# One whole block pair per feed-forward layer, all full norms by products with ones, and the norm's split moved

## The chip, the cores and the metric

The kernel runs on one core of a Trainium2 chip. The metric is device time in microseconds. The engines named below are PE (the matmul engine), DVE (vector), ACT (scalar), POOL (GpSimd) and SP (which issues the weight loads).

## What is computed

512 tokens of width 1024 pass through two chained models. The first has two layers: a gated recurrent mixer with memory attention (block A), then band attention with memory attention (block B), each followed by a feed-forward part with a causal convolution of three taps on the gate half. The second model has one layer (block C: two kinds of attention) and a plain gated feed-forward part. Every stage starts with a norm over the width. Cut to what matters here:

```
def rmsnorm(x, g):            # x32 * rsqrt(mean(x32 * x32) + eps) * g
def conv_ffn(h, w_up, conv_w, conv_b, w_down):        # layers 0 and 1, d_ff = 2816
    u, g = split(h @ w_up)
    g = g[t] * w2 + g[t-1] * w1 + g[t-2] * w0 + b     # causal_dwconv, k = 3
    return (silu(g) * u) @ w_down
second model, layer "2":      x = x + (silu(h2 @ w_gate) * (h2 @ w_up)) @ w_down
x = x + mixer(rmsnorm(x));  x = x + conv_ffn(rmsnorm(x));  k, v = rmsnorm(x, kv_g) @ w_kv
```

## The kernel before

**Layout.** Activations are held transposed, X[:, k, :] being features 128k to 128k+127 by 512 tokens. Every fp32 product is made of three products of rounded parts: high x high, high x low, low x high. The high part is a copy on ACT (`hH`, `WH`, `FH`, `TH`, `accH`), the low part a subtraction on DVE (`hL`, `WL`, `FL`, `TL`, `accL`). Weights come by SP's loads into `raw`; a unit of 2048 columns is converted in two halves (step `conv`), a chunk of 1024 in one (`cconv`).

**Feed-forward layers.** The 2816 hidden features are 11 block pairs of 256 gate and 256 up columns. The first WHOLE[i] pairs of layer i are computed whole: tiles g0, g1, u0, u1, each of 24 products of 512 columns (L1489; g1 in two halves, L1508, with the norm's products between). The other pairs use Winograd's form: seven products of half the width and half the depth (order 1, 5, 6, 3, 7, 2, 4; each 24 products of 256 columns, L1838). Their right operands are input sums T made by the steps `wtB`, `wtS`, `wtL` (four short DVE sums at L2557 to L2568, a copy, a low part at L2575; p = 0 to 3) and `wt7` (high and low of T7). Their left operands are weight blocks or sums of them (`wsum`, L2539, then `cconv`). Products 1, 6, 7, 4 share one PSUM bank: before 6, 7 and 4 the bank must be copied out by ACT (`wcopy`, tiles held, L2055); 5 and 3 share another. The down projection runs in pieces of 24 products (`wd`, L1864) that wait for the low part FL of the hidden tiles they read; ACT copies them out (`wx`) and POOL adds them to X by DMA.

**A whole pair's pointwise chain**: `wg0` (DVE, times the norm's R; in layers 0 and 1 then ACT's Identity with the last tap and the bias), `wt0` (in layers 0 and 1 two tap products per tile on DVE at L2601, then ACT's Silu), `wy0` (times R), `wu0` (times u; after the second tile ACT's FH), `wlast` (FL of the last whole pair).

**Norms.** ACT squares each X tile; POOL (in the residual steps of A, B, C and layer 0) or DVE adds the squares into acc. Two forms then follow. By rows (`row_split`, `row_sums`, `row_inverse`, for the names in ROW_NORMS): accH and accL, two PE products with a matrix of ones (L1378), a Sqrt over 128 x 512 on ACT (L2139), a reciprocal over 128 x 512 on DVE (L2734). By columns (`rstd_first`, `rstd_second`, used at n2): PE sums to four columns (L1371), a Sqrt and a reciprocal of 128 x 4, PE spreads them (L1383), ACT copies to Rsb.

**Order.** `order()` writes one list of steps, and each engine executes its own part of it strictly in that order; semaphores join the engines. `conv_ahead` puts conversions as far ahead as the four half-slots of converted weights allow. In a Winograd layer, `later(...)` lists groups of steps, and one group is put behind each product or down piece. `tile_done` puts norm steps and timed steps (gates) behind tiles. A `fence` makes the engines wait for each other's latest marked work; the one named acc2 stands ahead of layer 1, with a small load (graw) on ACT and a small weight copy on DVE (gw) behind it.

Of the kernel before, what the change touches and what calls it, by code (L numbers as in the profile page):

```python
# [10 lines left out]
ALU = mybir.AluOpType  # L11
# [22 lines left out]
NSU = 11  # L34
WHOLE = (2, 2, 1)
CHUNK = 1024
# [284 lines left out]
def pieces(hd):  # L321
# [3 lines left out]
    if hd % 2 == 0:  # L325
# [11 lines left out]
             "C": ([4, 5, 0, 1, 2, 3, 6, 7], 6)}  # L337
ROW_NORMS = ("ffn0", "kv", "ffn1")
NEXT_NORM = {"A": "ffn0", "B": "ffn1", "C": "n2"}
# [8 lines left out]
def order():  # L348
# [56 lines left out]
    def sink(*x):  # L405
        put(*x)
        if x[0] == "conv_in":
            deferred.append(("silu", x[1], x[2]))
        if x[0] == "gate":
            timed.extend([[1, ("gates_later",)], [3, ("gates_sums",)], [4, ("gates_rest",)], [6, ("gate_columns",)], [7, ("m_rows",)]])  # L410
        if x[0] == "fg":
            timed.extend([[0, ("fg_later",)], [1, ("fg_rest",)], [3, ("rows",)]])
        if x[0] == "rope":
            timed.append([1, ("rope_later", x[1], x[2])])
# [86 lines left out]
    def rstd(i, eps):  # L501
        norms.extend([("row_split", i), ("row_sums", i, eps), ("row_inverse", i)])

# [85 lines left out]
    def ffn_wino(i, end):  # L589
# [27 lines left out]
        def half(m, n, x):  # L617
            put("fm_half", f"g{i}", m, n, 128 * (m % 2), st, x)

        n = take()  # L620
        whole("g", 0, n)
        if st in ROW_NORMS:
            put("row_split", st)
            put("wtS", i, 1)
            half(1, n, 0)
            put("row_sums", st, 60)
            put("wtL", i, 1)
            half(1, n, 1)
            put("row_inverse", st)
            put("wtB", i, 2)  # L630
            put("wtS", i, 2)
        else:
            put("rstd_first", st, 61)
            put("wtS", i, 1)
            put("wtL", i, 1)
            put("wtB", i, 2)
            put("wtS", i, 2)
            whole("g", 1, n)
            put("rstd_second", st)
        done.add(n)  # L640
# [18 lines left out]
        if WHOLE[i] == 1:  # L659
            conv_ahead(len(UNITS))  # L660
            for m in (0, 1):
                put("wt0", f"g{i}", m)
            put("wy0", i, 0)
        conv_ahead(len(UNITS))
# [22 lines left out]
        if WHOLE[i] == 2:  # L687
            later([], [("wu0", f"u{i}", 3)], [("wt7", i)], [("wlast", i, 1)])
        else:
            later([("wt7", i)], [("wu0", f"u{i}", 0)], [("wu0", f"u{i}", 1)], [("wlast", i, 0)])  # L690
        for x in SEQUENCE[i]:
# [166 lines left out]
    ffn(0, "ffn0", "kv")  # L858
    put("sqrt_table", "kv")
    fm(1, "mix1", "qB", "R")  # L860
    put("fence", "kv")
# [147 lines left out]
def program(nc, wall, xt, memt, colsd, biasd, consts, rope, gatew, out):  # L1009
    ctx = ExitStack()  # L1010
    with ctx:
# [1450 lines left out]
        def vector(e):  # L2462
# [44 lines left out]
            for what, *a in STEPS:  # L2507
# [485 lines left out]
                elif what == "res_last":  # L2993
                    low_part(a[0], 7, col(a[0], 7))

                elif what == "g":
# [181 lines left out]
        def gpsimd(e):  # L3178
            w, mark = Lane(e), partial(ev.mark, "pool")

            for what, *a in STEPS:
# [66 lines left out]
                elif what == "res_norm":  # L3248
                    stage, m, st = a
                    if m:  # L3250
                        w.wait_ge(*at("sqA", st, m))
                        w.wait_ge(*(at("accP", st, m - 1) if m > 1 else at("sqA", st, 0)))
                        e.tensor_tensor(acc[:, :], acc[:, :], sq[m % 2][:, :], ALU.add).then_inc(
                            *mark("accP", st, m))
# [63 lines left out]
        def sync(e):  # L3318
# [34 lines left out]
            for h, k, n in STORES:  # L3353
# [9 lines left out]
        FFN_NEXT = ["kv", "n1", "last"]  # L3363
        SQ_LAST = {"mix0": "D", "ffn0": "P", "kv": "P", "ffn1": "P", "n2": "P", "last": "D"}
        R_OF["qmB"] = R_OF["qB"] = "kv"
# [7 lines left out]
        RCOL_USED = {"mix0": [], "kv": [("vev", "vA", 2, 2)], "n1": [("vev", "vB", 2, 2)],  # L3373
                     "n2": [("vev", "fv", 2, 1)], "last": [("spread", "n2")]}

# [129 lines left out]
```

## Time and profile before

| | us |
|---|---|
| median of 3 runs | 1774.73 (1773.79 to 1775.9) |
| profiled execution, its own time | 1773.94 |
| span of its trace | 1772.2 |
| PE busy | 1758.5 (99%) |
| DVE busy | 1293.8 (73%) |
| ACT busy | 950.0 (54%) |
| POOL busy | 205.3 (12%) |

PE's granted clock is full (0.999) over the span. In the rows, times are us from the span's start, then the duration; xN is a count; a bracket gives the idle time before the instruction and what released it. Busy PE time counts overlapping products; the distance between starts is the pace. Layer 0's feed-forward part starts at 260.2, layer 1's at 828.5, layer 2's at 1416.6; block B starts at 606.1, block C at 1177.5.

### The profile page before, as it was taken

To read this page: it belongs to the slowest core of one execution; us is meant where nothing else is said; L and a number is where in the kernel's file an instruction comes from. 1 tells how busy PE (TensorE), PEld (TensorE's weight loads), DVE (VectorE), ACT (ScalarE), POOL (GpSimd) and SP (SyncE) were. 2 spreads that over 40 slices of the span, in tenths; PEclk is the share of its full clock that TensorE was granted. 3 is DMA by queue.
4 is the path that set the end of the run, shared out by engine and by line. 5 is a ranking of instruction groups with operands and counts; after the bars stand their busy time and mean duration, and the time that the engine had idled before them with its cause. 6 is when DMAs were issued, how large, how long until landed. Compare 5 with 4: busy or idle time off the path is not lost.

```text
span 1772.2 us, 26238 instructions
## 1 busy us (share of the span) xinstructions
PE 1758.5 (99%) x10680; PEld 1525.7 (86%) x10680; DVE 1293.8 (73%) x1791; ACT 950.0 (54%) x1440; POOL 205.3 (12%) x226
## 2 busy tenths in 40 slices
PE   9999999999999999999999999999999999999998
PEld 7877788999999887787899999977777899999997
DVE  6878568888786765646888788689767487766766
ACT  6645444655554544754465555552567455454454
POOL 0001220110111200002011010103001101111110
PEclk9999999999999999999999999999999999999999
DMA  6231223654554342212264554443221235555442
GB/s 250 72 94 62 71 96 107 155 141 134 142 136 127 97 149 99 96 49 94 90 176 117 155 130 134 118 118 108 72 96 48 98 105 145 141 142 144 108 137 78
DMA packets 61623, 205.19 MB, mean 116 GB/s; under 512 B 7344, under 2 KB 9520, under 8 KB 53184
## 3 DMA queue, kind: packets, MB, share of 16 engines
q1 hardware_dynamic: 38832, 162.55, 27.6%
q0 software_dynamic: 17280, 31.46, 10.0%
q10 hardware_dynamic: 5392, 9.51, 1.7%
q8 instruction: 85, 1.39, 0.3%
q14 instruction: 34, 0.28, 0.0%
HBM read 169.38 MB, written 2.13 MB: 97 GB/s over the span
## 4 chain that ended last, share of the span: by engine, by line
PE 89%; DVE 6%; ACT 3%; issue 1%; DMA 1%; POOL 0%; ACTq 0%; DVEq 0%; SPq 0%; POOLq 0%
PE ps L1838 31%; PE ps L1489 17%; PE ps L1864 16%; PE ps L1403 6%; PE ps L1528 4%; PE ps L1651 2%; PE ps L1548 2%; PE ps L1696 2%; PE ps L1676 2%; DVE WL L2523 2%; PE ps L1735 1%; PE ps L1887 1%; PE ps L1716 1%; ACT WH L1978 1%; PE ps L1905 1%
## 5 line engine op out<-in xcount | busy, mean ns | idle before, releaser
L1838 PE MATMUL ps<-hH,WH 128*128 128x256 f32 x896 | 253.6, 283 | 0.7 <-ACT held L2055 0.7
L1838 PE MATMUL ps<-hH,WL 128*128 128x256 f32 x896 | 253.6, 283 | 0.0
L1838 PE MATMUL ps<-hL,WH 128*128 128x256 f32 x896 | 253.5, 283 | 0.0
L2545 DVE TENSOR_TENSOR WL<-raw,WH 128x1024 fp32r<-128x1024 f32 x138 | 168.1, 1220 | 112.8 <-ACT WH L1989 112.8
L2523 DVE TENSOR_TENSOR WL<-raw,WH 128x1024 fp32r<-128x1024 f32 (+1 forms) x137 | 169.4, 1275 | 83.8 <-ACT WH L1978 83.6
L1489 PE MATMUL ps<-hH,WH 128*128 128x512 f32 x528 | 208.3, 395 | 0.0
L1489 PE MATMUL ps<-hH,WL 128*128 128x512 f32 x528 | 205.7, 389 | 0.0
L1489 PE MATMUL ps<-hL,WH 128*128 128x512 f32 x528 | 205.6, 389 | 0.0
L3277 POOL DMA_DIRECT2D X<-sq x120 | 104.9, 964 | 862.4 <-ACT sq L2044 860.7
L1838 PE MATMUL ps<-TH,WL 128*128 128x256 f32 x672 | 190.2, 283 | 0.0
L1838 PE MATMUL ps<-TL,WH 128*128 128x256 f32 x672 | 190.2, 283 | 0.0
L1838 PE MATMUL ps<-TH,WH 128*128 128x256 f32 x672 | 190.1, 283 | 0.0
L2545 DVE TENSOR_TENSOR WL<-Wsum,WH 128x1024 fp32r<-128x1024 f32 x112 | 136.7, 1221 | 68.0 <-ACT WH L1989 67.9
L1978 ACT ACTIVATE WH<-raw 128x1024 fp32r<-128x1024 f32 (+1 forms) x137 | 134.4, 1028 | 83.9 <-PE ps L1489 44.2
L1838 PEld LDWEIGHTS ps<-hH,WH 128*128 128x128 f32 x896 | 171.9, 192 | 2.1 <-ACT held L2055 0.9
L1838 PEld LDWEIGHTS ps<-hL,WH 128*128 128x128 f32 x896 | 171.9, 192 | 1.2
L1838 PEld LDWEIGHTS ps<-hH,WL 128*128 128x128 f32 x896 | 171.9, 192 | 0.0
L1864 PE MATMUL ps<-FH,WH 128*128 128x512 f32 x432 | 168.7, 391 | 0.0
L1864 PE MATMUL ps<-FL,WH 128*128 128x512 f32 x432 | 168.7, 390 | 0.0
L1864 PE MATMUL ps<-FH,WL 128*128 128x512 f32 x432 | 168.1, 389 | 0.0
L1989 ACT ACTIVATE WH<-raw 128x1024 fp32r<-128x1024 f32 x138 | 144.5, 1053 | 18.7 <-PE ps L1838 16.5
L1989 ACT ACTIVATE WH<-Wsum 128x1024 fp32r<-128x1024 f32 x112 | 117.9, 1054 | 55.7 <-PE ps L1838 43.0
(442 smaller groups left out, 3890.8 us busy)
## 6 DMA issues: line engine op xcount, KB each, us to landing
raw<-in_wall SPq DMA_DIRECT2D x166, 512.0 KB, 4.4
raw<-in_wall SPq DMA_DIRECT2D x65, 1024.0 KB, 4.8
X<-sq POOLq DMA_DIRECT2D x120, 256.0 KB, 4.0
bias<-in_bias ACTq DMA_DIRECT2D x12, 256.0 KB, 2.9
raw<-in_wall SPq DMA_DIRECT2D x8, 256.0 KB, 6.6
X<-in_xt SPq DMA_DIRECT2D x8, 256.0 KB, 7.3
CB<-rows ACTq DMA_DIRECT2D x8, 256.0 KB, 3.3
out_y<-X SPq DMA_DIRECT2D x8, 256.0 KB, 2.2
```

What stands on the lines that cost most here:

```text
L1403: mm = e.matmul(ps[b][:, :], ww[:, k, c:c + 128], x, start=(k == seq[0] and i == 0), stop=(k == seq[-1] and i == 2))
L1489: mm = e.matmul(ps[b][:, 0:N], ww[:, k, c:c + 128], x[:, k, 0:N], start=(k == 0 and i == 0), stop=(k == 7 and i == 2))
L1528: mm = e.matmul(o, x[:, k, t * 128:t * 128 + 128], ww[:, k, :], start=(k == 0 and i == 0), stop=(k == 7 and i == 2))
L1548: mm = e.matmul(ps[b][:, :], x[:, k, t * 128:t * 128 + 128], ww[:, kx, :], start=(k == 0 and i == 0), stop=(k == 7 and i == 2))
L1651: mm = e.matmul(ps[b][:, c:c + L], queries[u["kind"]][r, u["m"], t * 128:t * 128 + 128], keys[u["kind"]][r, u["m"], 0:L], start=opens, sto ...
L1838: mm = e.matmul(ps[b][:, 256 * u:256 * u + 256], ww[:, p, 128 * u:128 * u + 128], x, start=(opens and p == 0 and u == 0 and n == 0), stop= ...
L1864: mm = e.matmul(ps[BANK["wd", i, g, m]][:, :], ww[:, kx, mi * 128:mi * 128 + 128], x[:, f % 8, :], start=(kx == 0 and n == 0), stop=(kx == ...
L1978: e.activation(WH[W_AT["unit", n] // 2][:, c], unit_raw(n)[:, c], ACT.Copy).then_inc(*mark("wh", n, x))
L1989: e.activation(chunk_slot(c)[0], chunk_src(c), ACT.Copy).then_inc(*mark("wh", "c", c))
L2523: e.tensor_tensor(WL[v][:, c], unit_raw(n)[:, c], WH[v][:, c].bitcast(F32), ALU.subtract).then_inc(*mark("wl", n, x))
L2545: e.tensor_tensor(L, chunk_src(c), H.bitcast(F32), ALU.subtract).then_inc(*mark("wl", "c", c))
L3277: e.dma_start(X[:, m, :], part[m % 2][:, :], accum_op=ALU.add).then_inc(s_part[m % 2], 16)
```

## The change

Layers 0 and 1 have one whole pair instead of two (layer 2 had one already), so ten Winograd blocks instead of nine. Their whole pair's taps, Silu, times R and times u are put behind the first Winograd products by `later`. The norm n2 is made by rows, as ffn0, ffn1 and kv were. At ffn0, ffn1 and n2 the last square is added by DVE instead of POOL, the split (accH, accL) stands ahead of the next unit's conversion instead of behind the first tile, and the Sqrt table is loaded ahead. At kv the split stands between the two halves of a conversion. The gate steps of block C (`fg_later`, `fg_rest`, `rows`) come one tile later.

```
-WHOLE = (2, 2, 1)
+WHOLE = (1, 1, 1)
-ROW_NORMS = ("ffn0", "kv", "ffn1")
+ROW_NORMS = ("ffn0", "kv", "ffn1", "n2")
-            timed.extend([[0, ("fg_later",)], [1, ("fg_rest",)], [3, ("rows",)]])
+            timed.extend([[1, ("fg_later",)], [2, ("fg_rest",)], [4, ("rows",)]])
     def rstd(i, eps):
-        norms.extend([("row_split", i), ("row_sums", i, eps), ("row_inverse", i)])
+        norms.extend([None, ("row_sums", i, eps), ("row_inverse", i)])
...
+        put("row_split", st)
         n = take()
+        put("sqrt_table", st)
         whole("g", 0, n)
-        if st in ROW_NORMS:
-            put("row_split", st)
-            ...
-        else:
-            put("rstd_first", st, 61)
-            ...
-            put("rstd_second", st)
+        put("wtS", i, 1)
+        half(1, n, 0)
+        put("row_sums", st, 61 if i == 2 else 60)
+        put("wtL", i, 1)
+        half(1, n, 1)
+        put("row_inverse", st)
+        put("wtB", i, 2)
+        put("wtS", i, 2)
         done.add(n)
         if WHOLE[i] == 1:
             sum_ahead(i)
...
         if WHOLE[i] == 1:
             conv_ahead(len(UNITS))
-            for m in (0, 1):
-                put("wt0", f"g{i}", m)
-            put("wy0", i, 0)
+            if i == 2:
+                for m in (0, 1):
+                    put("wt0", f"g{i}", m)
+                put("wy0", i, 0)
...
+        elif i == 2:
+            later([("wt7", i)], [("wu0", f"u{i}", 0)], [("wu0", f"u{i}", 1)], [("wlast", i, 0)])
         else:
-            later([("wt7", i)], [("wu0", f"u{i}", 0)], [("wu0", f"u{i}", 1)], [("wlast", i, 0)])
+            later([("wt7", i)], [("wt0", f"g{i}", 0), ("wt0", f"g{i}", 1)], [("wy0", i, 0), ("wu0", f"u{i}", 0)],
+                  [("wu0", f"u{i}", 1)], [("wlast", i, 0)])
...
     ffn(0, "ffn0", "kv")
     put("sqrt_table", "kv")
+    _, n = ITEMS[now["conv"]]
+    put("conv", n, 0)
+    put("row_split", "kv")
+    put("conv", n, 1)
+    now["conv"] += 1
     fm(1, "mix1", "qB", "R")
...
                 elif what == "res_last":                      # vector
                     low_part(a[0], 7, col(a[0], 7))
+                    w.wait_ge(*at("sqA", a[0], 7))
+                    w.wait_ge(*at("accP", a[0], 6))
+                    e.tensor_tensor(acc[:, :], acc[:, :], sq[1][:, :], ALU.add).then_inc(*mark("accD", a[0], 7))
...
                 elif what == "res_norm":                      # gpsimd
-                    if m:
+                    if 0 < m < 7:
```

The tables SQ_LAST and RCOL_USED follow (who adds the last square, and who last read the columns).

## Rows read from the trace of the kernel before

**Rows 1.** The page's first part: busy us, share, instructions.
```profile
PE 1758.5 (99%) x10680; PEld 1525.7 (86%) x10680; DVE 1293.8 (73%) x1791; ACT 950.0 (54%) x1440; POOL 205.3 (12%) x226
```
**Rows 2.** The chain of waits in order of time: start, us, what.
```profile
271.68 32.64 PE ps L1489 x144
...
394.66 14.39 PE ps L1838 x120
409.05 5.47 PE ps L1864 x24
```
**Rows 3.** Timeline of PE around norms and gates: start, us, what, idle before.
```profile
260.18 0.39 PE L1489 MATMUL ps<-hH,WH 128*128 128x512 f32 x1
...
268.34 0.39 PE L1378 MATMUL ps<-accH,ones_r 128*128 128x512 f32 x1
...
271.52 0.39 PE L1489 MATMUL ps<-hH,WH 128*128 128x512 f32 x1
...
617.98 0.47 PE L1378 MATMUL ps<-accH,ones_r 128*128 128x512 f32 x1 [0.86 <-DVE accL L2480]
...
838.62 0.47 PE L1378 MATMUL ps<-accH,ones_r 128*128 128x512 f32 x1 [1.82 <-DVE accL L2480]
...
889.50 0.39 PE L1838 MATMUL ps<-hH,WH 128*128 128x256 f32 x1 [0.72 <-ACT held L2055]
...
1197.63 1.02 PE L1915 MATMUL ps<-Gf,gsum 128*8 128x512 f32 x2 [0.62 <-DVE Gf L2467]
...
1416.57 0.39 PE L1489 MATMUL ps<-hH,WH 128*128 128x512 f32 x1
...
1429.21 0.48 PE L1489 MATMUL ps<-hH,WH 128*128 128x512 f32 x1
```
**Rows 4.** Windows: stretch, us, busy of PE, PEld, DVE, ACT, POOL, then clock, DMA.
```profile
304.00:335.00 31.00, 31.00 (x217) 29.07 (x216) 26.42 (x26) 18.49 (x26) 6.21 (x7) 1.00 0.57 136
...
1416.00:1440.00 24.00, 24.00 (x116) 20.11 (x115) 22.40 (x31) 11.66 (x16) 3.28 (x2) 1.00 0.26 88
```
**Rows 5.** Timelines of DVE and POOL at the kv norm and layer 1's.
```profile
617.15 0.69 DVE L2480 TENSOR_TENSOR accL<-acc,accH 128x512 fp32r<-128x512 f32 x1
...
830.00 3.41 POOL L3253 TENSOR_TENSOR acc<-acc,sq 128x512 f32<-128x512 f32 x2 [4.32 <-ACT sq L2330]
...
835.37 0.22 DVE L2772 TENSOR_TENSOR gw<-graw,gg 128x64 f32<-128x64 f32 x1 [1.61 <-DMA graw<-in_gatew]
...
837.79 0.68 DVE L2480 TENSOR_TENSOR accL<-acc,accH 128x512 fp32r<-128x512 f32 x1
```
**Rows 6.** Durations, from DVE's timeline and the page's groups (busy, mean ns, idle).
```profile
271.67 3.35 DVE L2734 RECIPROCAL Rsb<-Rsb 128x512 f32<-128x512 f32 x1 [1.04 <-ACT Rsb L2139]
...
282.75 2.98 DVE L2601 SCALAR_TENSOR_TENSOR yz<-gs,cols,yz 128x511 f32<-128x511 f32 x4 [0.29 <-ACT yz L2018]
...
1425.00 0.48 DVE L2568 SCALAR_TENSOR_TENSOR Tf<-X,small,Tf 128x256 f32<-128x256 f32 x1
...
L2545 DVE TENSOR_TENSOR WL<-raw,WH 128x1024 fp32r<-128x1024 f32 x138 | 168.1, 1220 | 112.8 <-ACT WH L1989 112.8
...
L1989 ACT ACTIVATE WH<-raw 128x1024 fp32r<-128x1024 f32 x138 | 144.5, 1053 | 18.7 <-PE ps L1838 16.5
```
**Rows 7.** Timelines of DVE, PE and ACT in the head of layer 2.
```profile
1420.26 3.45 DVE L2523 TENSOR_TENSOR WL<-raw,WH 128x1024 fp32r<-128x1024 f32 x2
...
1434.08 0.95 DVE L2575 TENSOR_TENSOR TL<-Tf,TH 128x768 fp32r<-128x768 f32 x1
1434.94 1.22 DVE L2545 TENSOR_TENSOR WL<-raw,WH 128x1024 fp32r<-128x1024 f32 x1
...
1440.19 0.28 PE L1838 MATMUL ps<-hH,WH 128*128 128x256 f32 x1
...
1442.50 1.28 ACT L2026 ACT_TABLE_LOAD   x1
1443.79 1.15 ACT L2026 ACTIVATE yz<-gs 128x512 f32<-128x512 f32 x2
```

## What was predicted

> **What bounds the kernel now.** I read the page first. PE is busy 99% of the span at full granted clock, the vector engine (DVE) 73% [rows 1]. The chain of waits is PE almost throughout, and in the steady part of a feed-forward layer nothing else appears: five Winograd products take 14.39 us, a down piece 5.47 [rows 2]. So the time can fall only by fewer PE columns or by closing one of the few PE gaps, and it rises by whatever makes PE wait. Then I read the PE timeline around the norms: the products with ones have no gap in layer 0, 0.86 us at the kv norm, 1.82 at layer 1 [rows 3]. Last, the window table: DVE is busy 26.4 of 31 us from 304 to 335 and 22.4 of 24 in the head of layer 2, which already has one whole pair [rows 4]. DVE is thus the engine to watch when work is pulled together.
>
> **PE work removed.** A whole pair is four tiles of 24 products, 96 x 0.2267 = 21.76 us (32.64 / 144 is the 0.2267). A Winograd block is seven times 24 half-width products, 7 x 2.878 = 20.15 us (14.39 / 5) [rows 2]. One pair is exchanged in layers 0 and 1: 1.61 x 2 = **-3.2 us**. The down pieces stay the same.
>
> **PE gaps closed.** Without a gap, two tiles and the two products with ones take 2 x 5.44 + 0.46 = 11.34 us: in layer 0 exactly from 260.18 to 271.52 [rows 2, 3]. A gap costs its idle time and about 0.24 for the refill: products of 0.39 us are issued 0.23 apart, so 0.16 of overlap is lost, and the first one after the gap takes 0.47 (0.08 more) [rows 3].
> Layer 1: 1.82 idle, 2.1 in all. The products wait for accL, which DVE makes at 837.79, behind two WL halves, themselves behind the small weight copy that waits for a DMA until 835.37 [rows 3, 5]. Now the seventh square is added by DVE (0.68) after the sixth, whose POOL add I put at 831.8, the middle of the 3.41 us for two; the graw load of ACT, now held by the fence until POOL's last add ends at 833.4 [rows 5], leaves about 0.6 us sooner (832.9) and lands near 834.75, and accL is next, done at 835.6. PE asks for it at 836.6. Gap gone: **-2.1**. The two WL halves behind it end at 837.9 and are wanted at 839.8: covered.
> Kv norm: 0.86 idle, 1.1 in all. Both splits now sit between the halves of the next conversion: accH after the first WH (614.83) and after POOL's last add, accL ends near 616.7 instead of 617.84 [rows 3, 5]. PE would ask for it near 617.0 (1.0 before 617.98). **-1.1**; the second WL half moves by 0.7 and is first read 2.7 us into the next tile.
> Layer 2: 1416.57 to 1429.21 is 12.64, with 16 small products; with the new form 11.34: **-1.3** [rows 3].
> Gate sums of block C: they move one tile (5.7 us) later, past Gf, so the 0.62 us gap [rows 3] closes: **-0.6** (the refill left out, since the two small products have one anyway). The Exp, Ln and the row store move with them by one tile; their reader is the fox part, tens of us later, so nothing is charged.
> A gap of 0.72 in layer 1 at 889.50 (q3 behind a held copy) [rows 3] lies in the stretch that is replaced: **-0.9** with the refill.
> Together **-9.2 us**.
>
> **What the change adds, in the DVE queue.** DVE and ACT run strictly in step order, so I lay the new order out, each item starting when the one before it ends (0.08 us overlap on DVE, 0.10 on ACT, as rows that follow each other show) or 0.04 after what it waits for; PE starts 0.15 after WL. Durations: a 1024-wide sum or low part 1.22, four T sums of 0.48 with their waits 1.75, the reciprocal 3.35, four taps 2.98, and on ACT a WH 1.05 [rows 6]; the 512-wide steps are half of these or a little more (0.68), a pair of 512-wide ones 1.28. Laid over the old order of layer 2, this gives 1434.7 for the end of the last TL, and the row has 1435.03 [rows 7].
>
> Layer 0, new order. DVE: low parts 6 and 7 to 262.6, square add to 263.2, ACT accH, accL to 264.6, two WL to 267.2, T sums to 268.9, TL 1 to 270.8, reciprocal to 274.0, T sums to 275.7, Wsum to 276.9, TL 2 to 277.7, T sums to 279.5, Wsum to 280.7, TL 3 to 281.5, WL of q1 to 282.7. PE has finished the u pair at 271.52 + 10.88 = 282.4 and starts q1 at 282.8: a wait of 0.4. Then WL q5, two gs, Wsum, WL q6 (0.9 late, ACT does the Identity pair first), Wsum, WL q3, L7, WL q7 to 292.7, the taps to 295.6. On ACT the step "taps behind the second copy" puts both Silus after held q5 and **ahead of** WH q2 and held q6: the second Silu ends at 296.2, WH q2 at 297.2, held q6 at 297.7. PE has done q1, q5, q6, q3 by 294.3, and q7 writes into the bank that held q6 empties: it starts at 297.8, a wait of **3.5**. q2 ends at 303.6. The down piece needs FL of the whole pair: DVE does WL q2 (298.4), times R (299.6), two u products (302.0, the d piece's WL between them); ACT FH to 303.1 and WH q4 to 304.1; DVE WL q4 to 305.4 and only then FL to 306.5. The piece starts at 306.6: a wait of **3.1**. In the old order the second whole pair (21.8 us of PE against some 13 us of DVE) paid for all this. After s = 1 DVE needs about 26 of 31 us per block [rows 4] and I find no further wait. Layer 0: **7.0 us**.
>
> Layer 1 is the same, but DVE stands at the weight copy until about 835.0, so WL q1 ends at 853.3 and PE is ready at 850.7: 2.8 + 3.5 + 3.1 = **9.4 us**.
>
> Layer 2 has no taps and kept its single pair; there WL q1 ended at 1436.16 and q1 began at 1440.19, 4.0 us of cover [rows 7]. The new norm adds to DVE the square add 0.6, accL with the wait for accH 1.4 and the reciprocal 3.35 - 0.16, while PE comes 1.4 us sooner; back come about 1.1 us that two WL lost beside POOL's add (3.45 us, where two of 1.22 take 2.36) and nearly as much in the low part before them [rows 6, 7]. The layout gives WL q1 at 1440.1 against PE at 1438.8: 1.4, and q6 waits 1.5 more for held q1, which ACT does behind a WH (waiting for its Wsum), the table load and two Silus. **2.9 us**.
>
> Bounds of these unshown waits: below, 0 in all, no wait, the old head of layer 2 being the nearest row; at durations 3% shorter I get 15.6 us, at 3% longer 22.8; the value taken is 19.3, since the same layout lags the old trace rather than leads it.
>
> ACT's table: the trace has the load at 1442.50 for 1.28 us and the next Silu at 1443.79 [rows 7]. The Trainium skill, "ScalarE: Activation LUTs" (What ACT_TABLE_LOAD costs), adds a drain of 1.38 us to every switch; here the next instruction follows at once. By the page the q6 wait of layer 2 would grow by 1.4 (in layers 0 and 1 the Silu waits for the taps anyway) and the time would be 1786.2; I go by the row.
>
> **Sum.** Own time of the profiled execution 1773.94 - 9.2 + 19.3 = 1784.0; the median of the runs lies 0.8 above that execution, so **1784.8 us**.
>
> **Rivals.**
> *The cover holds (faster).* No wait appears at the heads: 1774.7 - 9.2 = **1765.5**. For it: layer 2 ran its single whole pair without a PE gap, and DVE is idle 27% of the span [rows 1]. Against: that head had no taps (2.98), no reciprocal (3.35), and DVE was busy 22.4 of 24 us. It decides if the waits total under 9.2 us. Chance 0.10.
> *Half of them.* The q7 waits don't arise (held q6 gets through before the Silus) and layer 2 keeps its cover: 19.3 - 7.0 - 2.9 = 9.4 of waits, net +0.2: **1774.9**. Against: ACT executes in order, and the Silus stand first. Chance 0.08.
> *More waiting.* DVE or the loads run late: at 3% longer durations +13.6, and if the loads of the first parts gate Wsum (raw slots are released by the two WL that now end 0.8 later) another 1 to 2: **1789**. For it: the trace runs up to 1 us behind my layout near POOL adds. Against: POOL adds less now. Chance 0.17.
> *The gaps don't close* (the norm products still wait, because accL is late again): -9.2 shrinks by up to 3.2: **1788**. Chance 0.05.
> *The forecast:* 0.60, own range 1780 to 1788.
>
> **Range and chances.** The lower end takes in the half case, the upper the two worse ones: 1775 to 1790. Under 0.2% (3.5 us) a run can't be told from no change. Faster 0.11, same 0.07, slower 0.82.
>
> **What would show it.** Right: no PE gap at the products with ones at kv and layer 1; in layers 0 and 1 a PE gap of 3 to 4 us released by an ACT held copy before product 7 (the fifth in order), one of about 3 us before the first down piece released by DVE FL, a smaller one at q1; in layer 2 two of about 1.5; L1838 with 168 x 2 more products, L1489 with 96 x 2 fewer; POOL one add fewer at three norms. Wrong: heads without gaps, or DVE idle over 3 us between the reciprocal and the taps in layer 0; or new gaps in the middle of the layers, where I have none.

## The result, and the profile of the changed kernel

The changed kernel takes 1786.38 us (median of 4 runs, 1785.71 to 1787.97), the kernel before beside it 1774.26 (1773.02 to 1775.9): the ratio is 1.0071, 95% interval 1.006 to 1.0083. It is slower by 12.1 us. The forecast was 1784.8, that is 10.1 above the 1774.73 from which it started. A second measurement of the same kernel gave 1786.23 and 1.0067 [1.0055, 1.008].

The page's first part, to be held against [rows 1], and its slices of the granted clock:

```profile
PE 1761.6 (99%) x10810; PEld 1535.7 (86%) x10810; DVE 1316.2 (74%) x1813; ACT 961.1 (54%) x1455; POOL 202.5 (11%) x223
...
PEclk9999999999999999999899999999999999999999
```

PE is busy 3.1 us longer, though 3.2 us of its work were taken out: a product at a lower clock counts as busy for longer. One slice is an 8, the one that holds the head of layer 1. No slice of the kernel before was below 9. The counts are as forecast: 336 more products at the Winograd line (5040 for 4704); 216 fewer at the line of the whole tiles, of which 192 are the two pairs and 24 are layer 2's g1, now made in halves at another line; three adds fewer on POOL.

The PE timeline at the five places of [rows 3] and at the heads of the three feed-forward layers (start, us, what, idle before):

```profile
282.95 0.35 PE L1839 MATMUL ps<-hH,WH 128*128 128x256 f32 x1 [0.71 <-DVE WL L2546]
...
298.01 0.58 PE L1839 MATMUL ps<-hH,WH 128*128 128x256 f32 x1 [3.33 <-ACT held L2056]
...
307.04 0.47 PE L1865 MATMUL ps<-FH,WH 128*128 128x512 f32 x1 [1.50 <-DVE FL L2694]
...
622.43 0.39 PE L1379 MATMUL ps<-accH,ones_r 128*128 128x512 f32 x1
...
841.01 0.39 PE L1379 MATMUL ps<-accH,ones_r 128*128 128x512 f32 x1
...
858.48 0.56 PE L1839 MATMUL ps<-hH,WH 128*128 128x256 f32 x1 [3.26 <-DVE WL L2546]
...
873.54 0.39 PE L1839 MATMUL ps<-hH,WH 128*128 128x256 f32 x1 [0.59 <-ACT held L2056]
...
882.56 0.77 PE L1865 MATMUL ps<-FH,WH 128*128 128x512 f32 x1 [3.01 <-DVE FL L2694]
...
1214.96 1.03 PE L1916 MATMUL ps<-Gf,gsum 128*8 128x512 f32 x2
...
1452.43 0.36 PE L1839 MATMUL ps<-hH,WH 128*128 128x256 f32 x1 [1.60 <-DVE WL L2546]
...
1459.85 0.39 PE L1839 MATMUL ps<-TH,WH 128*128 128x256 f32 x1 [1.43 <-ACT held L2056]
```

A row without a bracket had no idle time before it: the gaps of 0.86 (kv norm), 1.82 (layer 1's norm) and 0.62 (gate sums) of [rows 3] are gone, and the 0.72 too. Eight new ones stand in the three heads: before product 1 (q1), before product 7 (q7; in layer 2 product 6), before the first down piece. Together 15.4 us.

Two of the queues behind these gaps, both in layer 0. ACT ahead of product 7: the second Silu, the WH of product 2, then the copy that product 7 waits for:

```profile
295.90 0.63 ACT L2027 ACTIVATE yz<-yz 128x512 f32<-128x512 f32 x1 [0.82 <-DVE yz L2602]
296.44 1.04 ACT L1990 ACTIVATE WH<-raw 128x1024 fp32r<-128x1024 f32 x1
297.38 0.58 ACT L2056 ACTIVATE held<-ps 128x512 f32<-128x512 f32 x1
```

DVE ahead of the first down piece: a WL that waits for ACT, then FL:

```profile
304.53 1.23 DVE L2546 TENSOR_TENSOR WL<-raw,WH 128x1024 fp32r<-128x1024 f32 x1 [1.54 <-ACT WH L1990]
305.67 1.22 DVE L2694 TENSOR_TENSOR FL<-yz,FH 128x1024 fp32r<-128x1024 f32 x1
```

What the gaps don't show is in the windows of the same kernel (stretch, us, busy of PE, PEld, DVE, ACT, POOL, granted clock, DMA share, GB/s):

```profile
290.00:298.00 8.00, 4.69 (x40) 4.48 (x38) 6.29 (x8) 5.16 (x8) 0.00 (x0) 1.00 0.39 131
298.00:307.00 9.00, 7.53 (x48) 7.33 (x48) 7.36 (x9) 4.34 (x5) 0.00 (x0) 0.81 0.46 123
...
858.00:862.00 4.00, 3.52 (x16) 3.55 (x17) 3.80 (x5) 1.89 (x3) 0.00 (x0) 0.50 0.00 0
862.00:866.00 4.00, 4.00 (x26) 4.00 (x25) 3.36 (x3) 3.54 (x5) 0.00 (x0) 0.67 0.02 4
866.00:870.00 4.00, 4.00 (x35) 4.00 (x35) 3.96 (x6) 2.37 (x4) 0.00 (x0) 1.00 0.78 262
882.00:886.00 4.00, 3.44 (x8) 2.80 (x9) 3.97 (x5) 1.06 (x1) 0.00 (x0) 0.50 0.45 131
886.00:891.00 5.00, 5.00 (x19) 4.00 (x19) 4.93 (x7) 2.49 (x4) 1.77 (x2) 0.75 0.11 20
```

A clock between 0.50 and 1.00 is the mean over a stretch that holds both levels. Behind each gap of 3 us the granted clock is at 0.50, the lower level of 1.2 GHz, and is back at 1.00 some 3 to 6 us after the gap. PE counts as busy there, but the window from 858, idle only in its first 0.48 us, holds 16 products where the one from 866 holds 35. The first four products of layer 1 took 14.47 us for 11.7 in layer 0, its first down piece 8.48 for 5.73.

By stage of the profiled execution: layer 0 +5.8 us, block B with the kv norm -1.1, layer 1 +8.2, block C -0.7, layer 2 to the end +2.1, the start -0.3. That is +14.0 in the span; this execution is the slowest of its four, 1.6 above their median.

### The profile page after: what moved, and what is told of

Read it like the earlier page. It is cut to its first block, busy times and chain, and to the rows that moved or that the text cites. A ratio compares the mean times of both kernels' runs of the same rounds, so it can differ in the third digit from the quotient of the medians.

```text
span 1786.2 us, 26555 instructions
## 1 busy us (share of the span) xinstructions
PE 1761.6 (99%) x10810; PEld 1535.7 (86%) x10810; DVE 1316.2 (74%) x1813; ACT 961.1 (54%) x1455; POOL 202.5 (11%) x223
## 4 chain that ended last, share of the span: by engine, by line
PE 88%; DVE 6%; ACT 3%; issue 1%; DMA 0%; DVEq 0%; SPq 0%; ACTq 0%
PE ps L1839 32%; PE ps L1865 17%; PE ps L1490 15%; PE ps L1404 5%; PE ps L1529 4%; PE ps L1888 3%; PE ps L1549 2%; PE ps L1652 2%; PE ps L1697 2%; PE ps L1677 2%; DVE WL L2524 1%; PE ps L1736 1%; DVE WL L2546 1%; PE ps L1717 1%; PE ps L1906 1%
## 5 line engine op out<-in xcount | busy, mean ns | idle before, releaser
L1839 PE MATMUL ps<-hH,WH 128*128 128x256 f32 x960 | 274.3, 286 | 9.5 <-DVE WL L2546 5.6
L1839 PE MATMUL ps<-hH,WL 128*128 128x256 f32 x960 | 273.8, 285 | 0.0
L1839 PE MATMUL ps<-hL,WH 128*128 128x256 f32 x960 | 273.8, 285 | 0.0
L1839 PE MATMUL ps<-TH,WH 128*128 128x256 f32 x720 | 204.3, 284 | 1.4 <-ACT held L2056 1.4
L1839 PEld LDWEIGHTS ps<-hH,WH 128*128 128x128 f32 x960 | 186.3, 194 | 12.1 <-issue 6.7
L1839 PEld LDWEIGHTS ps<-hL,WH 128*128 128x128 f32 x960 | 186.3, 194 | 1.0
L1839 PEld LDWEIGHTS ps<-hH,WL 128*128 128x128 f32 x960 | 186.3, 194 | 0.0
L1490 PE MATMUL ps<-hH,WH 128*128 128x512 f32 x456 | 180.4, 396 | 0.0
L1490 PE MATMUL ps<-hL,WH 128*128 128x512 f32 x456 | 177.9, 390 | 0.0
L1490 PE MATMUL ps<-hH,WL 128*128 128x512 f32 x456 | 177.8, 390 | 0.0
```

The source lines that it names most:

```text
L1490: mm = e.matmul(ps[b][:, 0:N], ww[:, k, c:c + 128], x[:, k, 0:N], start=(k == 0 and i == 0), stop=(k == 7 and i == 2))
L1839: mm = e.matmul(ps[b][:, 256 * u:256 * u + 256], ww[:, p, 128 * u:128 * u + 128], x, start=(opens and p == 0 and u == 0 and n == 0), stop= ...
```

## The experiments

Theory: the loss is the waits at the heads of the layers. They come from the order and the fullness of the DVE and ACT queues when one whole pair, not two, covers them, and the lowered clock behind them enlarges them. Rivals: the norm edits cost; the clock costs nothing of its own; DVE has no room in any order. Eleven variants and the changed kernel again were run. To compare them, this is the stretch from the end of the last u product to the end of the first down piece, in one profiled execution each, with one product (2.9) taken off where product 4 stands inside. The gaps are those before q1, before q7 and before the down piece, with the one before product 4 (q4) where it is named. Its work alone is 6 x 2.88 + 5.47 = 22.7 us.

| kernel | layer 0: gaps; stretch | layer 1: gaps; stretch | median us |
|---|---|---|---|
| changed | 0.71, 3.33, 1.50; 30.5 | 3.26, 0.59, 3.01; 35.8 | 1786.4 |
| changed_again | 0.71, 3.31, 1.56; 30.5 | 2.59, 1.83, 3.01; 33.9 | 1786.2 |
| pairs_only | 1.22, 3.32, 0.49; 31.0 | 0.64, 3.32, 0.39; 30.4 | 1785.1 |
| gate_load_later | 0.72, 3.31, 1.68; 30.5 | 1.68, 3.32, 0.41; 31.5 | 1784.3 |
| filled_gaps_layer1 | 0.73, 3.32, 1.53; 30.5 | 4.2 (filled 2.9), 1.76, 0.26; 32.4 | 1785.2 |
| taps_behind_q6 | 0.73, 0, 8.32; 34.1 | 2.68, 0, 6.83; 36.9 | 1792.7 |
| silus_behind_q6 | 0.72, 0, 4.84; 31.2 | 2.67, 0, 3.36; 32.2 | 1785.6 |
| taps_and_down_later | 0.73, 0, 5.43; 31.3 | 3.38, 0, 4.11; 33.6 | 1787.2 |
| order_mended | 0.72, 0, 2.83 (q4), 0; 28.2 | 1.62, 0, 2.84 (q4), 0; 30.3 | 1780.5 |
| mended_old_n2 | 0.72, 0, 2.84 (q4), 0; 28.2 | 1.68, 0, 2.84 (q4), 0; 29.2 | 1778.9 |
| mended_twice | 0.71, 0, 0, 1.55; 25.5 | 1.68, 0, 0, 1.53; 26.4 | 1778.6 |

**norms_only.** The norm edits and the new split order without the exchange in layers 0 and 1.

```
-WHOLE = (1, 1, 1)
+WHOLE = (2, 2, 1)
```

> The changed kernel with the split order and the norm edits, but layers 0 and 1 keep two whole pairs. Theory (the time is lost at the heads with one whole pair, the norm edits are worth what the gaps closed): block B -1.1, layer 1 norm -2.1, layer 2 norm form -1.3, gate sums -0.6, and the two new waits at the head of layer 2 +3.5 as the changed kernel's trace shows them: about 1.6 us under the kernel before, 1772.7. Rival (the norm edits themselves cost, by DVE work at the heads of all layers): above 1776. Rival (the whole loss comes from the pairs and layer 2's waits too need them): under 1770.5.

Measured 1773.68, ratio to the kernel before 0.9997 [0.9988, 1.0005], medians 0.9 us apart, which is not clear of the noise. The expectation was 1.6 faster; both rivals are out. Of the eight new gaps only layer 2's two are left, as PE's timeline shows:

```profile
1437.41 0.36 PE L1839 MATMUL ps<-hH,WH 128*128 128x256 f32 x1 [1.58 <-DVE WL L2546]
...
1444.82 0.39 PE L1839 MATMUL ps<-TH,WH 128*128 128x256 f32 x1 [1.43 <-ACT held L2056]
```

**norms_old_n2.** In addition layer 2's norm by columns again.

```
-ROW_NORMS = ("ffn0", "kv", "ffn1", "n2")
+ROW_NORMS = ("ffn0", "kv", "ffn1")
+        (for n2: rstd_first / rstd_second, last square on POOL, as before)
```

> As norms_only, and the norm of layer 2 again by small products over columns, its last square added by POOL. Theory: layer 2's two waits (3.5) and its gain (1.3) both go, so -1.1 -2.1 -0.6 = 3.8 us under the kernel before, 1770.5, and 2.2 under norms_only. Rival (layer 2's waits are not owed to its norm form): no difference from norms_only.

Measured 1771.04, ratio 0.9982 [0.9974, 0.9991]: 3.6 under the kernel before (3.8 expected) and 2.6 under norms_only (2.2). No gap over 0.05 us is left between 1400 and 1460. So layer 2's two waits belong to its new norm form, and this is the version that beats both kernels. No run takes the norm edits apart: whether the square on DVE or the earlier split closed layer 1's gap is not shown.

**pairs_only.** The exchange of the pairs alone, on the kernel before.

```
-WHOLE = (2, 2, 1)
+WHOLE = (1, 1, 1)
+        (taps and their followers by later(), as in the changed kernel)
```

> The kernel before with one whole pair in layers 0 and 1 and their taps behind the first product copies; norms and split order as before. Theory: the waits at the heads of layers 0 and 1 come from the order of the DVE and ACT queues there and stand without the norm edits: -1.6 x 2 - 0.9 + 7.9 + about 12 = +16, 1790. Rival (the waits need the norm edits, whose reciprocal and square add push the queue late): under 1782.

Measured 1785.11, ratio 1.0065 [1.0052, 1.0078]: +10.5, not +16, and not under 1782. The mechanism stands without the norm edits. Layer 0 lost 8.3 for 7.9 expected, layer 1 7.7 for 12. PE's timeline of this kernel, of layer 0 and of layer 1's norm:

```profile
298.94 0.58 PE L1842 MATMUL ps<-hH,WH 128*128 128x256 f32 x1 [3.32 <-ACT held L2059]
...
843.92 0.67 PE L1382 MATMUL ps<-accH,ones_r 128*128 128x512 f32 x1 [1.85 <-DVE accL L2484]
```

The norm's gap of 1.85 is there again, and behind it q1 of layer 1 waits only 0.64 us; in the changed kernel the norm has no gap and q1 waits 3.26 or 2.59. The two waits together are 2.5 us here and 2.6 or 3.3 there, so with one whole pair what is gained at that norm is given back at q1. That accounts for most of the 2.5 us by which the two parts alone, +10.5 and -0.9, fall short of the 12.1 of both.

**gate_load_later.** The small weight copy for which DVE stood still at layer 1's head is moved into the middle of the layer.

```
-    put("gg")
-    put("gate_weights", "C")
     ffn(1, "ffn1", None)
 ...
+            if (i, s, q) == (1, 2, 6):
+                put("gg")
+                put("gate_load", "C")
+            if (i, s, q) == (1, 2, 4):
+                put("gate_weights", "C")
```

> The changed kernel, but the small gate weights of block C are loaded and scaled in the middle of layer 1 and no longer at its head, so that DVE doesn't stand at 837.4 to 839.8. Theory (a PE gap of about 3 us is followed by a granted clock of 0.50 to 0.67, which costs again as much): WL of q1 comes 2.4 us sooner, the gap before q1 shrinks from 3.3 to about 0.8, PE stays at full clock there, and layer 1 loses what layer 0 does, 7.9 for 13.3: 5 us under the changed kernel, 1781. In the profile: granted clock 1.00 from 858 to 870, and the wait before q7 grows from 0.6 to about 3.3. Rival (the clock costs nothing of its own, only the wait counts): -2.4 or, as the later waits take it up, nothing: 1784 to 1786.

Measured 1784.25, ratio 1.0059 [1.0045, 1.0073]: 2 us under the changed kernel, neither 5 nor nothing. The profile has the things that the theory named, clock 1.00 from 858 to 870 and q7's wait at 3.3, but q1's gap shrank to 1.68 and not to 0.8. PE's timeline, then two windows:

```profile
857.19 0.36 PE L1842 MATMUL ps<-hH,WH 128*128 128x256 f32 x1 [1.68 <-DVE WL L2549]
...
872.25 0.58 PE L1842 MATMUL ps<-hH,WH 128*128 128x256 f32 x1 [3.32 <-ACT held L2059]
```

Columns as in the windows above:

```profile
858.00:862.00 4.00, 4.00 (x36) 4.00 (x35) 3.19 (x5) 3.18 (x4) 0.00 (x0) 1.00 0.01 4
...
870.00:876.00 6.00, 3.75 (x17) 3.75 (x18) 4.26 (x6) 3.00 (x4) 0.00 (x0) 0.61 0.29 87
```

The stretch is 31.5, 4.3 less than in the changed kernel's first profile but 2.4 less than in its second, which is nearer to its median. And the lowered clock moved with the gap, to q7: those 48 products took 8.62 us for 5.9. In the changed kernel DVE stood at the copy as long as this row says:

```profile
839.80 0.23 DVE L2773 TENSOR_TENSOR gw<-graw,gg 128x64 f32<-128x64 f32 x1 [2.44 <-DMA graw<-in_gatew]
```

Without it WL of q1 came 1.6 us sooner, counted from the layer's first product, and not 2.4, because DVE then waits 0.75 us for accH and 0.26 for a WH at the same place.

**changed_again.** The changed kernel once more, to see whether its clock was an accident.

> The changed kernel itself, word for word, beside the others of this call. Its profiled execution lay 1.6 us above its median, so part of the lowered clock in layer 1 may belong to that execution alone. Theory: gaps of 3 us or more always bring a lower clock behind them, but how much it costs changes between executions; median 1786 to 1787, and the profile of this run has granted clocks under 1.00 behind the same gaps. Rival: this profile has 1.00 there; then the lowered clock was an accident of one execution.

Measured 1786.23; the theory holds. The lower clock is behind the same two gaps, but shorter: 0.57 from 858 to 862 and 1.00 from there, 0.59 from 882 to 886. It cost 1.5 us at each where the first profile has 2.7. The gap at q1 is 0.7 shorter, and so is the time for which DVE stood at the weight copy: 1.71 us for 2.44, until its load landed. DVE's timeline:

```profile
839.38 0.23 DVE L2773 TENSOR_TENSOR gw<-graw,gg 128x64 f32<-128x64 f32 x1 [1.71 <-DMA graw<-in_gatew]
```

PE's:

```profile
858.06 0.55 PE L1839 MATMUL ps<-hH,WH 128*128 128x256 f32 x1 [2.59 <-DVE WL L2546]
```

And its windows:

```profile
858.00:862.00 4.00, 3.94 (x20) 3.97 (x21) 3.38 (x4) 2.31 (x3) 0.00 (x0) 0.57 0.00 0
862.00:866.00 4.00, 4.00 (x36) 4.00 (x35) 3.77 (x4) 3.83 (x6) 0.00 (x0) 1.00 0.15 19
```

**filled_gaps_layer1.** Products that nobody reads, where PE stood idle in layer 1 (the operands are abbreviated here).

```
+                    if (i, st, pn) == (1, 1, 1):
+                        w.wait_ge(*at("wh", "c", c))
+                        for n in range(24):
+                            e.matmul(ps[b][:, 0:256], WH of c [:, 0, 0:128], hH[:, 0, 0:256], start=True, stop=True)
 ...
+                        if (i, g, part) == (1, 0, 0) and pair == ms[0:2]:
+                            w.wait_ge(*at("wsilu", "H", i, 0))
+                            for n in range(12):
+                                e.matmul(ps[BANK["wd", i, g, ms[0]]][:, :], W[0][:, 0, 0:128], FH[:, 0, :], start=True, stop=True)
```

> The changed kernel with products that nobody reads, written into the bank that the real ones open afresh behind them: in layer 1, 24 of 128x256 before the wait for WL of q1 and 12 of 128x512 before the wait for FL of the first down piece. PE is busy where it stood idle, nothing else moves. Theory (the clock that falls behind a gap costs about 3 us twice in layer 1): granted clock 1.00 from 858 to 870 and from 882 to 891, 96 products in 11.7 us for 14.5, the down piece in 5.7 for 8.5; the wait before q7, which the slow products had hidden, grows from 0.6 to 3.3: together about 3 us less, 1783.3. Rival (the slow products only fill time that the waits take anyway): the stretch from u's end to the end of the down piece stays 36.0 us and the time 1786.

Measured 1785.24, ratio 1.0064 [1.0049, 1.0079]: 1.0 under the changed kernel's second measurement, less than the 3 expected and inside the spread of that kernel's executions (1784.32 to 1787.0), with these windows:

```profile
858.00:862.00 4.00, 4.00 (x36) 4.00 (x35) 3.40 (x4) 2.30 (x3) 0.00 (x0) 1.00 0.02 4
...
882.00:886.00 4.00, 3.84 (x17) 3.20 (x18) 3.96 (x5) 1.06 (x1) 0.00 (x0) 1.00 0.38 126
```

PE's timeline of the same kernel at q1, the filler and the first real product:

```profile
856.76 3.10 PE L1835 MATMUL ps<-hH,WH 128*128 128x256 f32 x24 [1.25 <-ACT WH L2001]
859.70 0.28 PE L1844 MATMUL ps<-hH,WH 128*128 128x256 f32 x1
```

The clock stays at 1.00, the 96 products take 11.7 and the down piece 5.7: that the clock has a price of its own is shown by these rows, not by the median. But the filler had to wait for WH until 856.76, and the first real product came at 859.70, 1.6 us later than in changed_again (858.06), which gave back half of the gain. Set against changed_again, the stretch is 1.5 shorter, and 3.1 without the overrun.

**taps_behind_q6.** Taps and Silus one step later, behind held q6 (layers 0 and 1).

```
-            later([("wt7", i)], [("wt0", f"g{i}", 0), ("wt0", f"g{i}", 1)], [("wy0", i, 0), ("wu0", f"u{i}", 0)],
+            later([("wt7", i)], [], [("wt0", f"g{i}", 0), ("wt0", f"g{i}", 1)], [("wy0", i, 0), ("wu0", f"u{i}", 0)],
```

> The changed kernel, but in layers 0 and 1 the four taps and two Silus of the whole pair stand one step later, behind the copy that empties product 6's bank (held q6); what follows them moves one step later too. Theory (the wait of 3.3 us before product 7 is only ACT's order): that wait is gone in both layers, but DVE has as much to do before FL, so most of it comes back before the first down piece, where 1.5 us (layer 0) and 3.0 (layer 1) become 4 to 5: 1784 to 1786, 0 to 2 under the changed kernel. Rival (each wait stands for itself): q7's 3.3 + 0.6 and the lowered clock behind them, some 2, are saved: 1780.

Measured 1792.72, ratio 1.0105 [1.0088, 1.0122]: 6 us slower than the changed kernel; both expectations fell. q7's wait is gone, as both said, but FL ended at 308.88 in place of 306.89, and PE stood 8.32 us before the down piece, then ran it at 0.50. The DVE timeline shows who is ahead of FL:

```profile
303.70 0.68 DVE L2618 TENSOR_TENSOR yz<-ps,yz 128x512 f32<-128x512 f32 x1
...
306.52 1.22 DVE L2546 TENSOR_TENSOR WL<-raw,WH 128x1024 fp32r<-128x1024 f32 x1 [0.99 <-ACT WH L1990]
307.66 1.22 DVE L2694 TENSOR_TENSOR FL<-yz,FH 128x1024 fp32r<-128x1024 f32 x1
```

ACT's timeline, with the row for which FL and the WH of that WL both wait:

```profile
304.48 1.06 ACT L2036 ACTIVATE FH<-yz 128x1024 fp32r<-128x1024 f32 x1 [4.18 <-DVE yz L2618]
```

A step later in the list is not one instruction later in the queue. A Wsum and a WL for the next block stand ahead of FL; but a WL that waits for ACT stood there in the changed kernel too, and FL begins 2.1 us behind the end of FH in both. What is new lies ahead of that: DVE did one more WL before the taps and a Winograd sum before the second product with u, which ran at 303.70 in place of 301.71. FH, that WL and FL each came 2.0 us later, while PE, without q7's wait and the slow clock, asked for FL 4.8 us earlier.

**taps_and_down_later.** The same, and the first down piece behind product 4.

```
+for x in SEQUENCE[:2]:
+    j = x.index(("d", 0, 0))
+    x[j:j + 2] = [x[j + 1], x[j]]
```

> As taps_behind_q6, and in layers 0 and 1 the first down piece stands behind product 4, so one more product (2.88 us) covers FL. Theory: no wait before product 7, at most 2 before the down piece, gaps of under 2 us with the clock kept at 1.00 in layer 0: 5 to 8 us under the changed kernel, 1780 with 1778 to 1782. Layer 1 keeps its wait of 3.3 at q1 and the lowered clock behind it. Rival (a DVE backlog that any order meets): within 2 us of the changed kernel.

Measured 1787.17, ratio 1.0074 [1.0059, 1.0089], the rival's answer: product 4 covers 2.9 of the 8.3, and FL, in the same queue, still ends at 308.82.

**silus_behind_q6.** On ACT alone; DVE's order is that of the changed kernel.

```
-            later([("wt7", i)], [("wt0", f"g{i}", 0), ("wt0", f"g{i}", 1)], [("wy0", i, 0), ("wu0", f"u{i}", 0)],
+            later([("wt7", i)], [("wt0", f"g{i}", 0), ("wt0", f"g{i}", 1)],
+                  [("ws0", f"g{i}", 0), ("ws0", f"g{i}", 1), ("wy0", i, 0), ("wu0", f"u{i}", 0)],
 ...
-                elif what == "wt0":     (ACT: the Silu; for layers 0 and 1)
+                elif what == ("wt0" if a[:1] == ["g2"] else "ws0"):
```

> The changed kernel with one thing moved, on ACT alone: the two Silus of the whole pair in layers 0 and 1 stand behind the copy that empties product 6's bank (held q6) in place of ahead of it. DVE's order is untouched. Theory: the wait of 3.3 us before product 7 goes, because it is ACT's order alone, and WL of q2 comes 1.5 us sooner; but FL stands behind a WL whose WH stands behind FH, so it ends near 305.2 in layer 0 where it ended at 306.9, and the first down piece waits 4.6 for 1.5. About 1.7 in each layer, 3 together: 1783. Rival (FL's end doesn't move, the wait only changes its place): 1786. Rival (all of the 3.3 is saved, with the clock): 1778.

Measured 1785.64, ratio 1.0069 [1.0056, 1.0081]. q7 starts without a wait, so that one was ACT's order alone: shown. FL ends at 305.72 and the gap is 4.84, as forecast (305.2, 4.6). DVE's timeline first:

```profile
303.35 1.23 DVE L2547 TENSOR_TENSOR WL<-raw,WH 128x1024 fp32r<-128x1024 f32 x1 [1.53 <-ACT WH L1991]
304.50 1.22 DVE L2695 TENSOR_TENSOR FL<-yz,FH 128x1024 fp32r<-128x1024 f32 x1
```

PE's timeline:

```profile
305.86 0.77 PE L1866 MATMUL ps<-FH,WH 128*128 128x512 f32 x1 [4.84 <-DVE FL L2695]
```

And the window behind that gap:

```profile
305.00:310.00 5.00, 4.14 (x10) 3.30 (x11) 4.97 (x6) 1.18 (x2) 0.00 (x0) 0.50 0.36 108
```

Yet only 0.6 us of the forecast 3 was saved. The clock is at 0.50 behind the one long gap, the down piece took 8.14 for 5.73, and that ate what FL had gained.

**order_mended.** In addition FL ahead of the next sums, the down piece behind product 4 (the edit of taps_and_down_later), the gate weights in mid-layer (the edit of gate_load_later).

```
-                  [("wu0", f"u{i}", 1)], [("wlast", i, 0)])
+                  [("wu0", f"u{i}", 1), ("wlast", i, 0)])
```

> silus_behind_q6, and in layers 0 and 1 FL ahead of the sums and low weights that follow it on DVE (right behind the pair's second product with u), the first down piece behind product 4, and the gate weights of block C in the middle of layer 1. Theory (every wait at these heads is order and backlog of DVE and ACT): q1 waits 0.7 in layer 0 and 1.7 in layer 1, q7 nothing, the down piece about 1 in each; clock 1.00 throughout; layers 0 and 1 lose 4.5 in all for 21.2 in the changed kernel (7.9 + 13.3): 16 us less, 1771. Rival (backlog: DVE has no room for the pair's work in any order, as with the taps moved whole): above 1780.

Measured 1780.49, ratio 1.0035 [1.0021, 1.0049]: 5.7 under the changed kernel, not 16. The waits for FL are gone, a new one stands before product 4, in both layers; PE's timeline in layer 0:

```profile
303.56 0.39 PE L1846 MATMUL ps<-TH,WH 128*128 128x256 f32 x1 [2.83 <-ACT held L2063]
```

ACT's timeline shows the same fault one copy further on:

```profile
301.02 1.06 ACT L2043 ACTIVATE FH<-yz 128x1024 fp32r<-128x1024 f32 x1 [3.28 <-DVE yz L2625]
301.99 1.04 ACT L1997 ACTIVATE WH<-raw 128x1024 fp32r<-128x1024 f32 x1
302.93 0.58 ACT L2063 ACTIVATE held<-ps 128x512 f32<-128x512 f32 x1
```

ACT stood idle for 3.28 us before FH, waiting for DVE, with the copy that PE needed behind it.

**mended_old_n2.** order_mended with layer 2's norm by columns.

> order_mended, with the norm of layer 2 over columns as in norms_old_n2. Theory: 2.2 under order_mended, 1769, which would be below norms_old_n2's 1771.0; the exchange of the pairs then pays its 1.6 in each layer less some 2 of waits, that is nearly nothing. Rival: layer waits as in order_mended's rival, above 1778.

Measured 1778.92, ratio 1.0028 [1.0017, 1.0039]: 1.6 under order_mended where 2.2 was expected. Of the two expected times it is the rival's, above 1778, since the layers still have the q4 waits of order_mended; it stands 7.9 above norms_old_n2.

**mended_twice.** On ACT, FH behind held q7.

```
+                  [("wu0", f"u{i}", 1), ("wlast", i, 0)], [("wf0", f"u{i}", 1)])
 ...
+                elif what == ("wu0" if a[:1] == ["u2"] else "wf0"):     (ACT: FH)
```

> mended_old_n2, and on ACT alone FH stands behind the copy that empties product 7's bank (held q7) in layers 0 and 1: that copy could leave near 298.3 in layer 0 and stood behind FH until 302.9, and product 4 waited 2.8 us for it in both layers. Theory: product 4 starts at once; the down piece then asks for FL and its own WL near 303.8, which end near 305.1, a gap of about 1.3; nearly 1.5 of wait less and 1 to 2.5 us of lowered clock less in each layer: 1778.9 - 6 = 1773, between 1771 and 1775. So one whole pair in layers 0 and 1 is worth nothing even when its worst waits are ordered away, against the 1771.0 of norms_old_n2. Rival (something behind it waits instead, as after each mend so far): 1777 or more.

Measured 1778.64, ratio 1.0026 [1.0015, 1.0037]: the rival's answer. The stretches are now 25.5 and 26.4 us, as the theory wanted, and q4 starts at once, but new waits stand behind it in both layers, 6.1 us in all (317.89 and 348.54, and 891.91 and 922.52):

```profile
305.11 0.51 PE L1883 MATMUL ps<-FH,WH 128*128 128x512 f32 x1 [1.55 <-DVE WL L2564]
...
317.89 0.39 PE L1857 MATMUL ps<-TH,WH 128*128 128x256 f32 x1 [1.26 <-ACT held L2074]
...
348.54 0.39 PE L1857 MATMUL ps<-hH,WH 128*128 128x256 f32 x1 [1.74 <-ACT held L2074]
```

Its profiled execution is the slowest of seven (1781.92 against the median), so the lost 4.8 us against the kernel before are not settled from it to the last microsecond.

## Why the prediction was right, and where it was not

- **PE work, -3.2.** Not visible by itself. With it layer 0's +5.8 is 7.8 lost in the stretch less 1.6, and 0.4 stays over.
- **Gaps closed, -6.0** (with the PE work these are the -9.2 of the forecast). All five went. By stage: block B -1.1 as forecast, block C -0.7 (0.6); layer 2 takes 11.34 us from its first product to the first of u, the figure forecast. norms_old_n2, which has three of them (kv, layer 1, gate sums), is 3.6 faster for a sum of 3.8. But pairs_only shows that layer 1's 2.1 is worth next to nothing with one whole pair, since q1 waits that much longer.
- **Layer 0, 7.0.** Lost 7.8. q1 0.71 (0.4), q7 3.33 (3.5, and by the cause named), the down piece 1.50 (3.1). This last term was mis-sized: FL ended at 306.89, where I had 306.5, but PE came at 305.5 and not at 303.6, since products 7 and 2 had run at a clock of 0.81 and taken 7.5 us for 5.9. Idle time and slow clock make 7.2 of the 7.8; the rest is the refill behind three gaps, which I charged where gaps closed and not where they opened.
- **Layer 1, 9.4.** Lost 13.1 in the first profile, 11.2 in the second. q1 3.26 and 2.59 (2.8), q7 0.59 and 1.83 (3.5), the down piece 3.01 (3.1). The q7 term failed in the good direction: slow products before it let ACT catch up. The 0.7 between the two values of q1 is the gate-weight load, for which DVE stood 2.44 and 1.71 us. The idle time is 2.5 and 2.0 under the forecast; the slow clock put 5.5 and 3.0 on top.
- **Layer 2, 2.9.** 1.60 and 1.43 for 1.4 and 1.5, and 0.5 of refill; norms_only and norms_old_n2 differ by 2.6 us, where the waits less the norm's gain should make 2.2.
- **The sum.** Idle at the heads is 15.4 us (16.0 in the second profile) for 19.3 forecast, and the lowered clock, for which there was no term, adds some 4.5 to 7. The refill of eight new gaps, at the 0.24 that the forecast itself gives for one, is another 1.9 at most and was left out too. The median came within 1.6 us of the forecast, and the rise within 2.0 (12.1 for 10.1), because the forecast's idle time, 3 to 4 us too long, stood against these two missing terms: where to wait and for whom was right, the total was right partly by luck.
- **The table load.** With a drain at each switch, layer 2's second wait would have been near 2.8; it is 1.43. The row before the load ends at 1456.85, and the Silu starts as the load ends. The rule of the Trainium skill, "ScalarE: Activation LUTs" (What ACT_TABLE_LOAD costs), which adds a drain of 1.38 us to a switch, is not borne out here:

```profile
1456.87 1.28 ACT L2027 ACT_TABLE_LOAD   x1
1458.16 1.15 ACT L2027 ACTIVATE yz<-gs 128x512 f32<-128x512 f32 x2
```

- **The rivals.** "The cover holds" took DVE's idle share for room. In the head of layer 0 that idle time (1.54 us before the WL ahead of FL, and 1.53 in silus_behind_q6) is DVE waiting for ACT. "More waiting" wanted DVE late; FL came 0.4 us after my layout.
- **What failed outside the forecast** were most of my later expectations. Of the eleven variants only norms_only and norms_old_n2 came within 1 us of the theory's time. pairs_only was 5 us faster than expected, filled_gaps_layer1, silus_behind_q6 and gate_load_later 2 to 3 slower, and taps_behind_q6, taps_and_down_later, order_mended, mended_old_n2 and mended_twice 6 to 10 slower. In silus_behind_q6 the queue was laid out right (a gap of 4.84 for 4.6) and only the clock behind the gap was missing. In the five large misses (mended_old_n2 takes over the order of order_mended) I removed the wait that the profile named and did not lay out the whole queue behind it again.

What stays open: why the lowered clock lasts some 6 us behind a gap in one execution and 3 to 4 in another of the same kernel; and whether an order exists in which the exchange gains its 1.6 us per layer. The reordering took 7.6 us off, with layer 2's old norm in it, and left it 7.6 above norms_old_n2.

## What to carry to other kernels

When work that covers a queue is exchanged for work that needs the queue sooner, write the queue of each helper engine down in order, every instruction of it, and read off when the ones that PE waits for end; the saving on PE (here 1.6 us a layer) is small against one wait. An instruction that must wait, put ahead of the copy that frees PE's bank, can cost PE the whole wait (3.3 us at q7, 2.8 at q4): order an in-order engine by who is waited for. Price a PE gap of about 3 us at its length and half to as much again, and measure parts of a change alone: here three closed gaps were worth keeping (1771.0), the rest not.

## What the runs showed of the hardware

I had no lowered clock in the forecast, with gaps of 3.5 us in it. By gap before the products, and the granted clock in the profile's rows for the 4 to 10 us behind it: 1.55 us 1.00; 1.68 1.00; 1.76 (filled_gaps_layer1) 1.00; 1.82 (kernel before, [rows 3]) 1.00; 1.83 (changed_again) 1.00; 1.74 and 1.84 (mended_twice at 348.5 and 922.5) 0.72; 1.85 (pairs_only at 843.9) 0.66; 2.59 0.57; 2.83 0.66; 3.3 0.81 (layer 0, the changed kernel) and 0.53 (pairs_only, layer 1); 3.01 to 3.26 0.50 (the changed kernel's first profile; 0.59 behind 3.01 in its second); 4.84 0.50; 8.32 0.50. So every gap from 2.59 us up had the lower level behind it, and of the six from 1.74 to 1.85 three had and three had not. It costs 1.5 to 3 us each time, and not the same in each execution: one kernel, mended_twice, ran at 1777.0 to 1779.1 us five times with a mean clock of 0.999 and at 1781.2 and 1781.9 with 0.997. The window of pairs_only behind its gap of 1.85, which the kernel before had at 1.82 and full clock:

```profile
843.00:848.00 5.00, 4.08 (x11) 3.28 (x12) 3.41 (x7) 2.45 (x3) 0.00 (x0) 0.66 0.64 211
```

That a PE that does nothing loses half its clock is what the Trainium skill says in "TensorE: Matmul & The Clock Gate" (What's actually happening), "the default state is throttled, and activity releases the throttle"; the traces agree, at 0.50.
